# First norm by quarters, bias rows by groups of heads, and second-block products taken from unscaled tokens

## What is computed

```python
# first block
mod = silu(c) @ w_ada + b_ada                 # one row of 6 x 1024
sh1, sc1, g1, sh2, sc2, g2 = split(mod, 6)
h = rms_norm(x, norm1_g) * (1 + sc1) + sh1
proj = h @ w_in                               # retention q, k, v, gate; attention; branch gates
bias = rel_bias[t5_bucket(distance)]          # 3 groups of 4 attention heads, added to the scores
x = x + g1 * token_mixer(...)
x = x + g2 * relu(h2 @ w1)**2 @ w2            # h2: second norm
x = rms_norm(x, norm_f_g)
# second block, first of two layers
p = x @ w_in_2[0]                             # then MLA, mLSTM and SSD on parts of p
x = layernorm(ALPHA * x + mix, ...)
```

## Time and profile before

| | us |
|---|---|
| median of 3 runs | 1362.06 (1361.8 to 1364.44) |
| the profiled execution | 1361.76 |
| its span, first to last instruction | 1360.0 |
| TensorE busy | 1304.6 |
| VectorE, ACT, GpSimd busy | 888.4, 736.3, 641.2 |

### The profile page before, as it was taken

One profiled execution on the slowest core, in us unless ns is written; L12 is line 12 of the kernel. 1 busy time (PEld: TensorE's weight loads), 2 busy tenths in 40 slices (PEclk: granted clock), 3 DMA queues, 4 the chain that ended last, 5 costly groups with the idle time before them and its releaser, 6 DMA issues.

```text
span 1360.0 us, 18658 instructions
## 1 busy us (share of the span) xinstructions
PE 1304.6 (96%) x6684; PEld 1083.6 (80%) x6684; DVE 888.4 (65%) x1383; ACT 736.3 (54%) x1107; POOL 641.2 (47%) x512
## 2 busy tenths in 40 slices
PE   7999999999999999999999999999989999899997
PEld 4778788899887788888787887888868787788885
DVE  6783884354444564214678667888867867788777
ACT  5343454344464444445566437666745663667664
POOL 3898899988868699998400420000060034000000
PEclk9999999999999999999999999999999999999999
DMA  9868468746544455555531018878854300688782
GB/s 373 318 261 309 155 246 318 247 156 248 191 150 170 169 186 186 186 188 184 215 126 63 1 51 314 311 282 326 292 189 168 104 22 1 232 309 299 285 311 94
DMA packets 45496, 280.03 MB, mean 206 GB/s; under 512 B 5565, under 2 KB 8893, under 8 KB 13918
## 3 DMA queue, kind: packets, MB, share of 16 engines
q1 hardware_dynamic: 38434, 263.82, 53.5%
q10 hardware_dynamic: 6974, 15.05, 3.1%
HBM read 274.66 MB, written 4.19 MB: 205 GB/s over the span
## 4 chain that ended last, share of the span: by engine, by line
PE 73%; DVE 12%; POOL 5%; DVEq 4%; ACT 3%; issue 2%; DMA 1%; ACTq 1%; SPq 0%; POOLq 0%
PE AC L1315 9%; PE AC L1317 9%; PE AC L1316 9%; PE G L1315 8%; PE G L1317 8%; PE G L1316 8%; POOL w_lo L721 5%; PE T L1507 2%; PE G L1507 2%; DVE w_lo L2195 2%; PE G L1353 1%; PE G L1352 1%; PE G L1351 1%; PE T L1508 1%; PE G L1508 1%
## 5 line engine op out<-in xcount | busy, mean ns | idle before, releaser
L721 POOL TENSOR_TENSOR w_lo<-w_raw,w_hi 128x512 fp32r<-128x512 f32 (+1 forms) x470 | 611.6, 1337 | 322.3 <-ACT w_hi L784 311.2
L784 ACT ACTIVATE w_hi<-w_raw 128x1024 fp32r<-128x1024 f32 x444 | 467.3, 1059 | 391.2 <-PE AC L1317 165.4
L2195 DVE TENSOR_TENSOR w_lo<-w_raw,w_hi 128x1024 fp32r<-128x1024 f32 x228 | 275.6, 1223 | 52.7 <-ACT w_hi L784 44.4
L1315 PE MATMUL AC<-w_hi,yT_hi 128*128 128x512 f32 x368 | 145.3, 395 | 0.9 <-POOL w_lo L721 0.9
L1317 PE MATMUL AC<-w_hi,yT_lo 128*128 128x512 f32 x368 | 142.7, 388 | 0.0
L1316 PE MATMUL AC<-w_lo,yT_hi 128*128 128x512 f32 x368 | 142.6, 387 | 0.0
L1315 PE MATMUL G<-w_hi,arena_r 128*128 128x512 f32 x320 | 128.2, 401 | 4.4 <-DVE w_lo L3065 2.3
L1317 PE MATMUL G<-w_hi,arena_r 128*128 128x512 f32 x320 | 125.1, 391 | 0.0
L1316 PE MATMUL G<-w_lo,arena_r 128*128 128x512 f32 x320 | 124.8, 390 | 0.0
L1315 PE MATMUL G<-w_hi,xT 128*128 128x512 f32 (+1 forms) x240 | 98.4, 410 | 5.6 <-DVE xT L2347 2.1
L1315 PE MATMUL AC<-w_hi,xT 128*128 128x512 f32 x240 | 97.5, 406 | 3.3 <-POOL w_lo L721 2.3
(11 more groups left out here) (514 smaller groups left out, 2537.5 us busy)
## 6 DMA issues: line engine op xcount, KB each, us to landing
w_raw<-w_stream SPq DMA_DIRECT2D x148, 1024.0 KB, 5.1
w_raw<-w_expert SPq DMA_DIRECT2D x94, 1024.0 KB, 5.2
arena<-w_stream SPq DMA_DIRECT2D x8, 512.0 KB, 12.1
mod<-rows ACTq DMA_DIRECT2D x2, 2048.0 KB, 9.1
rel_scratch<-arena ACTq DMA_DIRECT2D x1, 3072.0 KB, 12.7
w_raw<-w_expert SPq DMA_DIRECT2D x4, 512.0 KB, 4.4
mod<-rows ACTq DMA_DIRECT2D x3, 476.0 KB, 3.9
x_sb<-x SPq DMA_DIRECT2D x1, 1024.0 KB, 8.3
```

The source lines that it names most:

```text
L721: i = pool.tensor_tensor(w_lo[:, k % SLOTS, cols], w_raw[:, raw, cols], w_hi[:, k % SLOTS, cols].bitcast(F32), ALU.subtract)
L784: act.activation(w_hi[:, k % SLOTS, :], w_raw[:, raw, :], ACT.Copy).then_inc(hi_ready, 1)
L1315: pe.matmul(out, xh, wh, start=start, stop=False)
L2195: dve.tensor_tensor(w_lo[:, k % SLOTS, :], w_raw[:, k % RAW, :], w_hi[:, k % SLOTS, :].bitcast(F32), ALU.subtract).then_inc(lo_ready, 1)
```

## The change

1. **The first norm goes by quarters** of 256 columns. x is scaled by its inverse root alone (ACT), turned at once, and gain and shift are applied after the turning, where they are one number for each partition. So the modulation is needed as columns: the sums over partitions are matmuls with one output column (`quarter_sums`). VectorE's sums for a quarter are eight operations of 128x512 with the accumulator in PSUM (`ada_quarter`). TensorE computes only chunk 7 of quarter 0.
2. **Units are reordered** so that each quarter serves all three tiles: quarter 0 of tiles 0, 1, 2, then quarter 1, and so on. SyncE's order and the places of the later modulation pieces change (`ADA_AFTER`), VectorE's list `DVE_LO` too.
3. **Bias rows** are made for four heads at once on four partitions, three pairs of matmuls; a small store writes them, and three DMAs from DRAM to DRAM on ACT's queue copy each to 128 rows.
4. **The second block's first layer** takes its products from x before the final norm's scale for each token: x_sb is turned as soon as the residual is in; the gain is applied by column when the high and low halves are made; the scale for the token is applied when the products are read from PSUM. The second token tile is turned after two units.

```diff
-ADA_DVE = (range(0, KC), range(3, KC))
-ADA_PE = range(0, 3)
...
+QUARTERS = 4
+QC = KC // QUARTERS
+QW = 2 * QC * P
+ADA_FIRST = QUARTERS * KC
+N_SUMMED = QUARTERS - 2
+PE_SUM = KC - 1
+ADA_AFTER = {18: 1, 22: 2, 26: 3, 30: 4, 34: 5, 40: 6, 46: 7, 52: 8, 56: 9, 60: 10, 66: 11, 72: 12, 78: 13, 84: 14, 90: 15}
+DVE_LO = [U_RET_IN + 10, U_RET_IN + 11] + [U_RET_IN + UP * j - 1 for j in (11, 12, 13)]
...
-    return U_RET_IN + 2 * PRE * (u // 2) + 2 * j + u % 2
+    return U_RET_IN + PRE * u + j
...
-            sp.dma_start(ccol, A["c_col"]).then_inc(c_loaded, 16)
-            for s in range(n_ring):
...
+            sp.dma_start(sm[:, 336:336 + 4 * KC], A["c_col"]).then_inc(c_loaded, 16)
+            sp.dma_start(x_sb[:, :, :], A["x"].rearrange("b (t p) d -> p (b t) d", p=P)).then_inc(x_loaded, 16)
             sp.dma_start(ident[:, :], A["identity"]).then_inc(ident_loaded, 16)
-            def first_weights(s):
...
+            piece(0, 2)
+            piece(1, 3)
+            def first_units(s):
+                for u in range(PIECE):
+                    sp.dma_start(w_raw[:, s * PIECE + u, :], A["w_stream"][2 * n_ring + s][:, u * UNIT:(u + 1) * UNIT]).then_inc(raw_landed[s], 16)
+            def quarter(q):
+                for h in range(2):
+                    sp.dma_start(quarter_home[2 * q + h], A["w_stream"][2 * q + h]).then_inc(quarter_landed[2 * (q % 2) + h], 16)
+            first_units(0)
+            quarter(1)
+            first_units(1)
+            sp.wait_ge(ada_used, KC // 2)
+            piece(2 * n_ring + 2, 2)
+            quarter(2)
+            lows_done(PIECE)
+            piece(3 * n_ring, 0)
+            sp.wait_ge(ada_used, 2 * KC)
+            quarter(3)
+            lows_done(2 * PIECE)
+            piece(3 * n_ring + 1, 1)
             sp.dma_start(arena[:, 19968:20480], A["const1"][:, 1536:2048]).then_inc(cst_loaded, 16)
             sp.wait_ge(ada_used, KC)
             piece(3 * n_ring - 1, n_ring - 1)
             sp.dma_start(inv_row, A["inv_freq"].partition_broadcast(P)).then_inc(pos_loaded, 16)
             sp.dma_start(pos_i[:, :], A["pos_col"]).then_inc(pos_loaded, 16)
+            def ada_piece(i):
...
-                if k == 1:
-                    pool.wait_ge(h_ready, TOK)
...
+            def turn_hi_gained(n, t):
+                for b in range(HALVES):
+                    act.wait_ge(t_ready, n + b + 1)
+                    for c in range(4 * b, 4 * b + 4):
+                        i = act.activation(xT_hi[:, c, t * P:(t + 1) * P], T[:, b, (c - 4 * b) * P:(c - 4 * b + 1) * P], ACT.Copy, scale=normf_col[:, c:c + 1])
+                    i.then_inc(t_hi, 1)
...
+            act.wait_ge(rstd_done, 1)
+            for t in range(TOK):
+                act.activation(xs[:, t, :], x_sb[:, t, :], ACT.Copy, scale=var[t]).then_inc(h_ready, HALVES)
+            def turned_quarter(q):
+                for i in range(QC):
+                    act.wait_ge(h_turned, QC * q + i + 1)
+                    act.activation(xT_hi[:, QC * q + i, :], h_full[:, i * S:(i + 1) * S], ACT.Copy).then_inc(chunk_hi, 1)
+            his(U_RET_IN, U_RET_IN + 2)
+            turned_quarter(0)
+            for g in range(len(GROUPS)):
+                act.wait_ge(bias_row, g + 1)
+                act.activation(bias_vec[:, g, :], row_banks[g], ACT.Copy).then_inc(bias_rows_out, 1)
+            his(U_RET_IN + 2, U_RET_IN + PRE + 2)
+            for q in range(1, QUARTERS):
+                turned_quarter(q)
+                his(U_RET_IN + PRE * q + 2, U_RET_IN + min(PRE * (q + 1) + 2, PRE * UP - 1))
+            act.wait_ge(bias_rows_out, len(GROUPS))
+            act.dma_start(A["rel_scratch"][:, P, :].rearrange("(g h) n -> h g n", h=AH), bias_vec).then_inc(bias_stored, 16)
             def early_after(j):
...
+                if j in (7, 9, 11):
+                    g = (j - 7) // 2
+                    heads = slice(g * AH, (g + 1) * AH)
+                    act.wait_ge(bias_stored, 16)
+                    act.dma_start(A["rel_scratch"][heads, 0:P, :], A["rel_scratch"][heads, P:P + 1, :].to_broadcast([AH, P, NT])).then_inc(bias_stored, 16)
...
+            act.wait_ge(bias_stored, 64)
...
-                turn_hi_x(t + LT_X, 0)
+                    square(HALVES * TOK, 1, 1)
+                    turn_hi_gained(t + (LT_X + 2), 1)
+                    root(R_FINAL, var[0])
+                    root(r, var[1])
+                else:
+                    turn_hi_x(t + LT_X, 0)
+                    his(SLOTS - 1, SLOTS, n)
+                    root(r, var[1])
...
-                    if u == UP - 1:
+                    if u == second:
...
+            def quarter_turn(q):
+                for i in range(QC):
+                    for t in range(TOK):
+                        c = QC * q + i
+                        pe.transpose(turn_bank(q)[:, i * S + t * P:i * S + (t + 1) * P], xs[:, t, c * P:(c + 1) * P], ident[:, :])
+            def quarter_sums(q):
+                pe.wait_ge(ada_summed, q + 1)
+                for i in range(2 * QC):
+                    o = pe.matmul(sum_cols(q)[:, i:i + 1], mod1[:, q, i * P:(i + 1) * P], ones_col, start=True, stop=True)
+                o.then_inc(scale_sum, 1)
+            for g in range(len(GROUPS)):
+                bias_rows_of(g)
+            pe.wait_ge(ident_loaded, 16)
+            keep_busy(G[:, 0, :], 7)
+            pe.wait_ge(c_ready, 1)
+            pe.wait_ge(raw_landed[3], 16)
+            for i in range(2 * QC):
+                at = (PE_SUM - KC // 2) * QW + i * P
+                o = pe.matmul(G[:, 1, i:i + 1], quarter_home[1][:, at:at + P], csil[:, PE_SUM:PE_SUM + 1], start=True, stop=True)
+            o.then_inc(scale_sum, 1)
+            pe.wait_ge(h_ready, HALVES * TOK)
+            quarter_turn(0)
+            quarter_sums(0)
+            keep_busy(G[:, 0, :], 8)
...
-                    for u in (2 * c, 2 * c + 1):
-                        k = first_unit(j, u)
...
+                    k = first_unit(j, u)
+                    if u == 0 and j == 1:
+                        pe.wait_ge(bias_rows_out, len(GROUPS))
+                    if j == PRE - 1 and u + 1 < QUARTERS:
+                        quarter_sums(u + 1)
+                    low_half(0, k)
+                    for t in range(TOK):
+                        for q in range(QC):
+                            ch, w = QC * u + q, slice(q * NT, (q + 1) * NT)
+                            if (j, t) == (0, 0):
+                                pe.wait_ge(chunk_lo, ch + 1)
+                            i = mm3(pre_banks[j][:, t, :], xT_hi[:, ch, t * P:(t + 1) * P], xT_lo[:, ch, t * P:(t + 1) * P],
+                                    w_hi[:, k % SLOTS, w], w_lo[:, k % SLOTS, w], ch == 0, ch == KC - 1)
+                    i.then_inc(unit_used, 1)
+                    if j == 0 and u + 1 < QUARTERS:
+                        quarter_turn(u + 1)
             for j in range(PRE - 1, N_RET_IN):
                 if j >= PRE:
...
+                    up_normed(n, L_IN, G, tb + LT_X, x_sb, res_ready, HALVES * TOK, width=FIRST, second=UP // HALVES)
...
+            def ada_quarter(q, s0, s1):
+                last = KC - 1 if q else PE_SUM - 1
+                for s in range(s0, s1):
+                    h = s // (KC // 2)
+                    if s % (KC // 2) == 0:
+                        dve.wait_ge(quarter_landed[2 * (q % 2) + h] if q else raw_landed[2 + h], 32 if q == 3 else 16)
+                    w = quarter_home[2 * q + h][:, s % (KC // 2) * QW:(s % (KC // 2) + 1) * QW]
+                    if s == 0:
+                        dve.tensor_scalar(mod1[:, q, :], w, csil[:, 0:1], None, ALU.mult).then_inc(ada_used, 1)
                     else:
-                        dve.wait_ge(half_landed[s // PIECE], 16 * PIECE)
-                    dve.scalar_tensor_tensor(m, half_home[s] if c else w_raw[:, s, :], csil[:, s:s + 1], m, ALU.mult, ALU.add).then_inc(ada_used, 1)
+                        dve.scalar_tensor_tensor(sum_bank(q) if s < last else mod1[:, q, :], w, csil[:, s:s + 1],
+                                                 sum_bank(q) if s > 1 else mod1[:, q, :], ALU.mult, ALU.add).then_inc(ada_used, 1)
...
+            rstd(0, sm[:, 16:18], 1.0 / D, 1e-6, lambda: ada_quarter(0, 0, 1))
+            dve.memset(sm[:, 892:893], 0.0).then_inc(rstd_done, 1)
+            ada_quarter(0, 1, PE_SUM)
+            dve.wait_ge(scale_sum, 1)
+            dve.tensor_tensor(b_col[:, 0:2 * QC], G[:, 1, 0:2 * QC], b_col[:, 0:2 * QC], ALU.add).then_inc(ada_used, 1)
+            dep()
+            def turned_quarter(q):
+                cols, b = slice(QC * q, QC * (q + 1)), b_col[:, 2 * QC * q:2 * QC * (q + 1)]
+                dve.wait_ge(scale_sum, q + 2)
+                dve.tensor_tensor(b, sum_cols(q), b, ALU.add)
+                dep()
+                dve.tensor_tensor(a_col[:, cols], b[:, QC:2 * QC], g_col[:, cols], ALU.mult)
+                dep()
+                for i in range(QC):
+                    c = QC * q + i
```

(61 more changed lines are left out.)

249 lines of the change are left out of this document (88 added, 161 removed).

## The result

The changed kernel took 1366.92 us (median; 1362.25 to 1368.45 in 11 runs), the kernel before 1361.8 beside it: a ratio of 1.0032, 95% interval 1.0022 to 1.0041. It is slower by 0.3%, where 11.0 us of gain were forecast. The profiled execution took 1362.25 us (span 1360.5), the lowest of its runs and 4.7 us under their median, so its trace shows a mild case of what went wrong; where the other executions lose the rest is in no trace. Rows come from it unless another kernel is named.

What follows compares the result with a forecast made beforehand. TensorE, busy 1304.6 of 1360.0 us, was taken as the bound, with time to win only in its stops, half clock and non-product work. 9.4 + 1.4 - 2.8 + 3.3 - 0.3 = 11.0 us off 1362.06 gave 1351.0, range 1346 to 1358.

Steps and rivals of the forecast that it cites:

- Bias rows and their copies: Narrow copies, small store and three DRAM broadcasts replace twelve copies and a 3 MB store: counted nothing, up to 3 us uncovered.
- Parts A and B: Kernel start to the first product, then to the thirteenth weight unit: 9.4 us gained together, bounds 5 and 11.5.
- First product: TensorE's first product on the first block's input: at 19.3 us, 9.1 us earlier; bounds 18 and 22.
- Thirteenth unit: Start of the thirteenth weight unit in the first block: 62.9 us instead of 72.26, after twelve units ending at 60.3.
- the wait on the rotation: Before the thirteenth unit: TensorE waits for VectorE's PSUM reads of rotations 0 and 1, the latter ending at 62.5 us.
- VectorE's quarter sums: First norm: 0.69 us each, 0.77 with drain, eight per quarter; above 1 us the forecast is wrong.
- ACT's high halves waited for DMA in the first 60 us: Sign at the start, named as showing the forecast wrong; no size given.
- Part C: TensorE's waits on GpSimd from 72 to 112 us, 2.0 in all: 1.4 us gained, 0 to 2.0.
- Part D: Modulation sums moved into the first group norm delay VectorE's low halves; wait at 190.06 grows: 2.8 us lost, 0 to 3.3.
- Part E: Step between the blocks, x_sb turned before scaling: 3.3 us gained, bounds 1.5 and 4.5; other scaled reads cost 0.3.
- The sum: Whole kernel, all terms together: 11.0 us gained, 1362.06 to 1351.0 us.
- The cold first quarter: Rival at the start: all 36 first-quarter products at 0.43 us, 7.3 us where 1.6 was counted, giving 1356.7; chance 0.10.

Runs made afterwards that it cites:

- late6: `spread_busy` with VectorE's two sums of modulation piece 6 put behind its gate product and the awaited low half: 1353.23 us, ratio 0.9948 to the kernel before.
- boundary_only: The kernel before with Part E's new step between the blocks alone: 1362.88 us, ratio 1.0001.
- spread_copies: The changed kernel with the three bias-row broadcasts described with 128 rows outermost (the spread kernel): 1355.67 us, ratio 0.9961 to the kernel before.
- spread_busy: `spread_copies` plus filler: seven pairs of passes between the blocks, four before the second block's gate rows: 1353.27 us, ratio 0.9921 to the kernel before.
- all: `late6` with five filler pairs for eight before the first product and gate-row filler in both layers: 1353.16 us, ratio 0.9940 to the kernel before.
- fill5: `spread_busy` with five pairs of filler passes instead of eight right ahead of the first product: 1354.34 us, ratio 0.9951 to the kernel before.

## Why the prediction was wrong

**Bias rows and their copies: this step failed.** It said that the broadcasts run while the DMA is half free, that the last has 9 us until ACT needs it, and counted nothing, at most 3. It took the mean free share of sixteen engines for room that a copy on four of them could use: 1 MB needs about 11 us alone (the estimate above) and took 20.7 from issue to ACT's release. The price in the trace is 8.9 us (from 6.8 ahead to 2.1 behind) and 1.8 of low clock; over 11 and 6 runs, unspread and spread copies differ by 0.71%, 9.7 us. No rival had it.

**Parts A and B: right in sum, off in the first term.** First product at 21.26, not 19.3 (bounds 18 to 22): VectorE's first low part took 1.55 us beside GpSimd, where 0.43 was put down, and the column sums before it were done at 17.66, with 1.87 us for the 1.0 that was counted. x and the two pieces landed within 0.3 us of the forecast. Thirteenth unit at 62.75, forecast 62.9, with the wait on the rotation that was named: the twelve units were done at 61.3 instead of 60.3, and that wait, 1.42 us where the forecast left 2.6, hid it. That the sum came out all the same is in part luck. VectorE's quarter sums took 0.755, 0.83 with the drain, forecast 0.69 and 0.77. One sign that it had named for being wrong did come: ACT's high halves waited for DMA in the first 60 us, 1.83, 1.18 and 3.30 us (the last at 47.16), but TensorE stood behind none of them. Two of its sums are off: 3.5 MB at 0.42 MB/us are 8.3 us, not 8.8, and nine matmuls 0.2 us longer 1.8, not 1.6.

**Part C: all of it, by a wrong count.** No wait on GpSimd from 62 to 112 us; the lead grew by 2.3 us over the earlier trace rows's stretch, 1.4 forecast. The 2.0 us of rows 7 hold the 0.78 that ends at 72.26, which A and B had already counted. The 1.2 us that are left gave 2.3, since each stop that went was worth 0.2 to 0.3 us more than its recorded idle time (the one of 0.30 at 75.57 gave 0.6).

**Part D: a wait came, but elsewhere and for another reason.** The product at 190.06 before, whose wait was to grow to near 4 us, starts at 182.20 in the changed kernel with no wait. The wait for VectorE's low half (2.32 us at 169.59) came one listed unit earlier, at the counterpart of the first row; the low half itself is the second and third row, before and after:

```profile
178.00 0.39 PE L1315 MATMUL G<-w_hi,xT 128*128 128x512 f32 x1
172.94 2.31 DVE L2278 TENSOR_TENSOR w_lo<-w_raw,w_hi 128x1024 fp32r<-128x1024 f32 x1
167.25 2.28 DVE L2322 TENSOR_TENSOR w_lo<-w_raw,w_hi 128x1024 fp32r<-128x1024 f32 x1
```
Before, it was done 2.75 us ahead of TensorE; now TensorE comes 10.9 us earlier and VectorE 5.7. The wait stays when piece 4 is moved back, and `late6` shows that piece 6's sums make it. Their place in VectorE's order is unchanged, but they now wait 1.50 us for their weights. The move itself is a gain of some 3.4 us, since at its old place VectorE stands for weights. From 85.58 to 191.83 the lead fell by 5.0 us, more than the 2.8 counted: the wait of 2.32 and the low clock behind it cost 4.2 (the products from 170.22 to 173.21 start 0.43 apart), those of 0.45 and 1.00 cost 0.8 and 1.3, and the 1.01 that the kernel before has in that stretch gives 1.3 back.

**Part E: right where the clock holds.** 3.0 us in the trace and 2.9 by the ratios, forecast 3.3 less 0.3. Not foreseen was that arriving earlier changes whether the clock falls 70 us later, which takes nearly all of it in `boundary_only` and in the spread kernel.

**The sum.** With the failed step mended the change gives 5.3 us by the ratio (`spread_copies`), about half of the 11.0. Its trace leads by 7.2 us before the blocks meet and by 9.2 after, and the clock takes 1.9 of that. Filler, which is no part of the change, gives some of it back: 10.8 us in all by the ratio of `spread_busy`, but 7.1 and 8.2 by those of `late6` and `all`, which hold the same filler, and 8.4 by the end of its trace. So that the 11.0 of the sum was there is not shown. The bias copies had a term, put at nothing; the falls of the clock behind the first layer had none. The cold first quarter of the rivals did not occur in the changed kernel (four slow products, 0.8 us); `fill5`, with three pairs of filler fewer, had twelve, a third of the rival's 36.

## What to carry to other kernels

A DMA's own rate comes before the share of the DMA that is free: read the slowest dimension of both its patterns, and where that is 4, count it at a quarter of the rate and on engines that it shares. Put the 128 rows outermost, and don't issue a four-row copy right behind another from an engine with other work.

A gain ahead of a stretch of short matmuls and short waits may be lost there to the clock. Look at the granted clock of each later stretch before counting on the gain, and fill the longest wait; then look again, since the fall may only move (here to 1086 us).

Moving a sum behind other work can be a gain where its engine stood for the sum's operand at the old place: read who ends the wait there, not only what the sum takes.

The mean of a merged row says nothing of its first instruction: of two low parts that last 1.88 us together the first, which TensorE waited for, took 1.55.

## What the runs showed of the hardware

A DMA's issue can hold its engine: 8.57 and 11.40 us for a broadcast issued 13 to 15 us after another on the same four DMA engines, 0.54 to 0.65 when spread over 128 rows. The held issues ended at 122.2 and 139.9 us, while packets of the copy before ran on until 132.7 and 150.4, so it was not the end of that copy that they waited for. What held them was not separated.

In the first unit of `fill5` products started 0.43 us apart, the pace of 1.2 GHz, while the clock column showed 1.00 for 21 to 24 us:

```profile
21.00:24.00 3.00, 2.80 (x7) 1.00 1.05 441
```
For short stretches at the start the pace of equal matmuls tells the level better than the clock column does.

A stop of TensorE cost 0.2 to 0.3 us more than its recorded idle time (0.30 recorded and 0.6 gained when it went, 0.45 and 0.8 when it came).
